# Shift and scale of a conditioned encoder layer in two parts of 512 features, the first six W_in blocks in two halves of K

## What is computed

```
mod = (silu(c) @ w_mod + b_mod).reshape(B, 6, 1, D)
shift1, scale1, gate1 = mod[:, 0], mod[:, 1], mod[:, 2]
h  = layer_norm(x) * (1 + scale1) + shift1
z  = h @ w_in + b_in            # [u | v | pool | gates], 5 * 1024 columns
v  = gelu(z_v) ...
```

## Time and profile before

| | us |
|---|---|
| median of 3 runs | 949.63 |
| lowest, highest | 948.38, 950.42 |
| the profiled execution | 948.7 |
| its span, first to last instruction | 947.0 |
| PE busy | 897.3 (95%) |
| DVE, ACT, POOL busy | 379.0, 241.4, 114.2 |
| mean granted clock of TensorE | 0.990 |

### The profile page before, as it was taken

The page is one execution under the profiler, slowest core; times in us unless marked ns, Lnnn a source line. Parts: engine busy times, 40 slices in busy tenths (PEclk is TensorE's granted clock), DMA queues, the critical chain, the costliest instruction groups (busy, mean ns, idle before and its releaser), DMA issues. The chain is left out here.

```text
span 947.0 us, 11855 instructions
## 1 busy us (share of the span) xinstructions
PE 897.3 (95%) x4416; PEld 543.0 (57%) x4416; DVE 379.0 (40%) x647; ACT 241.4 (25%) x351; POOL 114.2 (12%) x143
## 2 busy tenths in 40 slices
PE   3999999999999999999999999999888999999994
PEld 2577766888888888787544444344344344444431
DVE  4533443466344236788622323132121232222346
ACT  2422243441234235345511111011010011101113
POOL 2120366000001000000000000000000010000041
PEclk9999999999999999999999999999998999999998
DMA  9985755356464722807999999999999999999994
GB/s 369 357 269 183 265 190 183 118 190 253 178 225 157 219 89 89 300 11 310 401 385 415 425 420 428 421 428 424 427 424 420 414 405 425 423 427 423 424 415 144
DMA packets 53126, 295.27 MB, mean 312 GB/s; under 512 B 5606, under 2 KB 7750, under 8 KB 33602
## 3 DMA queue, kind: packets, MB, share of 16 engines
q1 hardware_dynamic: 42752, 263.47, 69.3%
q0 software_dynamic: 9824, 29.80, 9.3%
q10 hardware_dynamic: 482, 1.13, 0.3%
HBM read 275.81 MB, written 22.83 MB: 315 GB/s over the span
## 5 line engine op out<-in xcount | busy, mean ns | idle before, releaser
L674 PE MATMUL banks<-down_w,hid_t 128*64 128x512 f32 x512 | 118.5, 599 | 10.7 <-issue 5.9
L674 PE MATMUL banks<-h_hi,w_hi 128*128 128x512 f32 x320 | 124.8, 390 | 0.3 <-ACT h_hi L1287 0.3
L674 PE MATMUL banks<-h_hi,w_lo 128*128 128x512 f32 x320 | 124.7, 390 | 0.0
L674 PE MATMUL banks<-h_lo,w_hi 128*128 128x512 f32 x320 | 124.6, 397 | 0.0
L674 PE MATMUL banks<-up_w,x_by_expert 128*64 128x512 f32 x256 | 112.5, 592 | 0.0
L674 PE MATMUL banks<-gate_w,x_by_expert 128*64 128x512 f32 x256 | 112.5, 592 | 0.0
L674 PE MATMUL banks<-gate_w,x_by_pair 128*64 128x512 f32 x240 | 105.5, 592 | 0.1
L674 PE MATMUL banks<-up_w,x_by_pair 128*64 128x512 f32 x240 | 105.5, 592 | 0.0
L1673 DVE TENSOR_TENSOR w_lo<-raw,w_hi 128x1024 fp32r<-128x1024 f32 x56 | 68.5, 1225 | 77.2 <-ACT w_hi L1253 77.1
L1493 ACT ACTIVATE sg_hid<-banks 64x512 f32<-64x512 f32 x33 | 19.5, 591 | 311.6 <-PE banks L674 311.6
L2019 DVE TENSOR_TENSOR sg_hid<-banks,sg_hid 64x512 f32<-64x512 f32 x32 | 22.2, 694 | 183.8 <-ACT sg_hid L1493 183.7
(11 more groups left out here) (325 smaller groups left out, 1304.6 us busy)
## 6 DMA issues: line engine op xcount, KB each, us to landing
down_w<-in_w_exp_down SPq DMA_DIRECT2D x64, 1024.0 KB, 18.2
gate_w<-in_w_exp_gate SPq DMA_DIRECT2D x28, 2048.0 KB, 21.1
up_w<-in_w_exp_up SPq DMA_DIRECT2D x28, 2048.0 KB, 25.6
modraw<-in_w_mod SPq DMA_DIRECT2D x24, 1024.0 KB, 7.7
raw<-in_w_in SPq DMA_DIRECT2D x9, 2048.0 KB, 9.8
round_y<-zrow POOLq DMA_DIRECT2D x6, 2048.0 KB, 7.7
gate_w<-in_w_exp_gate SPq DMA_DIRECT2D x6, 1024.0 KB, 9.5
up_w<-in_w_exp_up SPq DMA_DIRECT2D x6, 1024.0 KB, 12.0
```

Of the source, the lines that this page charges most:

```text
L674: return pe.matmul(out, lhsT, rhs, start=start, stop=stop, skip_group_check=True)
```

## The change

The 1024 features of shift1 and scale1 are computed in two parts of 512.

- W_mod's first 2048 columns are loaded in two rounds of eight loads (first_mod_source): part 0 takes columns 0 to 511 of shift and of scale for all 1024 rows, part 1 columns 512 to 1023. A load is 512 KB in runs of 2 KB. Behind part 0 come the chunks 0 to 3 of W_in unit 0 (in two pieces of 256 columns) and of unit 1; behind part 1 the chunks 4 to 7 of both.
- A modulation unit (first_mod_unit) handles two chunks of rows; a part has four units of four products each. Even and odd chunks are summed in different rows of MOD, and VectorE adds the two when it takes the columns (first_scales). So 16 + 16 products stand where 32 stood, and two sets of column transposes where one stood. They go to bank 7.
- h is formed for chunks 0 to 3 behind part 0, and for 4 to 7 behind part 1 (H_VECTOR = 2, 0, 6, 4; H_POOL = 1, 3, 5, 7; H_ORDER is gone).
- Blocks 0 to 5 are summed in six banks, first over chunks 0 to 3, then over 4 to 7. Their splits use four half buffers. TensorE's order: pair of blocks 0 and 1 over part 0; unit (1,0); block 2; unit (1,1); block 3; units (1,2) and (1,3); block 4; columns of part 1; block 5; the pair over part 1; then the loop n = 0 to 7, in which blocks 2 to 5 have only their second half.
- On VectorE the copy of the parameters' columns (pcol) moves behind the scaling of x; the silu waits for TensorE directly. b_mod comes by 12 DMAs instead of 8. One keep_clock(512) stands between units (0,2) and (0,3), where three stood around units 6 and 7.

```diff
-            for m in range(KC):
-                if m == 6:
-                    sp.dma_start(raw[:, 0, :, 0:256], unit_source(0)[:, :, 0:256]).then_inc(s_wfirst, 16)
-                sp.dma_start(modraw0[m][:, :, :], mod_source(m)).then_inc(s_m0[m], 16)
-            sp.dma_start(raw[:, 0, :, 256:512], unit_source(0)[:, :, 256:512]).then_inc(s_w[0], 16)
-            load_unit(1)
+            for part in range(2):
+                for kc in range(KC):
+                    m = 4 * part + kc // 2
+                    landed = s_m0[4 + kc // 4 if part else kc // 2]
+                    sp.dma_start(modraw0[m][:, kc % 2, :, :], first_mod_source(part, kc)).then_inc(landed, 16)
+                chunks = slice(PART * part, PART * part + PART)
+                if part == 0:
+                    for c in range(2):
+                        cols = slice(256 * c, 256 * c + 256)
+                        sp.dma_start(raw[:, 0, chunks, cols], unit_source(0)[:, chunks, cols]).then_inc(s_wpre[c], 16)
+                    sp.dma_start(raw[:, 1, chunks, :], unit_source(1)[:, chunks, :]).then_inc(s_wpre[2], 16)
+                else:
+                    for u in range(2):
+                        sp.dma_start(raw[:, u, chunks, :], unit_source(u)[:, chunks, :]).then_inc(s_w[u], 16)
...
+            def first_mod_unit(part, q):
+                if part == 0:
+                    pe.wait_ge(s_m0[q], 32)
+                else:
+                    pe.wait_ge(s_m0[4 + q // 2], 64)
+                for k in range(2):
+                    for v in range(2):
+                        j = 2 * v + k
+                        x = mm(MOD[32 * j:32 * j + 32, :], silu_c[:, 2 * q + k, :], modraw0[4 * part + q][:, k, v, :], start=(q == 0), stop=(q == 3))
+                x.then_inc(pe_mod, 1)
...
-            mod_units0(0, 2)
+            first_mod_unit(0, 0)
+            first_mod_unit(0, 1)
...
-            mod_units0(2, KC)
+            first_mod_unit(0, 2)
+            keep_clock(512)
+            first_mod_unit(0, 3)
             keep_clock(256)
             pe.wait_ge(act_nt, 2 * TILES)
...
+            part_pair(0)
+            first_mod_unit(1, 0)
+            part_block(0, 2)
+            first_mod_unit(1, 1)
+            part_block(0, 3)
+            first_mod_unit(1, 2)
+            first_mod_unit(1, 3)
+            part_block(0, 4)
+            pe.wait_ge(dve_col, 1)
+            first_mod_columns(1)
+            part_block(0, 5)
+            part_pair(1)
             for n in range(8):
-                if n >= 2:
+                if 2 <= n < FIRST:
+                    part_block(1, n)
+                elif n >= FIRST:
                     block_at(n, n % 2, h_hi, h_lo, act_z, n - 1)
...
-            dve.wait_ge(pe_pro, 1)
-            dve.tensor_copy(pcol[:, :], COL[:, 0:64]).then_inc(dve_pro, 1)
...
+            first_mod_rows(0)
+            first_scales(0)
+            dve.wait_ge(dve_col, 2)
+            first_split_lo(0)
+            first_split_lo(1)
+            for kc in H_VECTOR[0:2]:
+                modulated(kc)
+            for kc in range(PART):
+                h_low(kc)
+            for b in range(2, FIRST):
+                first_split_lo(b)
+            first_mod_rows(1)
+            split_lo(0)
+            split_lo(1)
+            first_scales(1)
+            dve.wait_ge(dve_col, 4)
+            for kc in H_VECTOR[2:4]:
+                modulated(kc)
+            for kc in range(PART, KC):
+                h_low(kc)
```

More of the change, by code:

```diff
@@ L211, in hybrid_encoder @@
         s_sgu_w = sem("s_sgu_w")
-        s_wfirst = sem("s_wfirst")
+        s_wpre = [sem(f"s_wpre{i}") for i in range(3)]
         s_bmod = sem("s_bmod")
-        s_m0 = [sem(f"s_m0_{i}") for i in range(KC)]
+        s_m0 = [sem(f"s_m0_{i}") for i in range(6)]
         s_m = [sem(f"s_m{i}") for i in range(2)]
@@ L371, in mod_source, with first_mod_source, halves_of_chunks, bank_of @@
             return w_mod[0, kc * 128:kc * 128 + 128, r * 2048:r * 2048 + 2048].rearrange("p (j n) -> p j n", j=4)
+        def first_mod_source(part, kc):
+            return w_mod[0, 128 * kc:128 * kc + 128, 0:2048].rearrange("p (v f n) -> p v f n", v=2, f=2)[:, :, part, :]
+        def halves_of_chunks(tiles, turn):
+            first = PART * (turn // 2 % 2)
+            return tiles[turn % 2][:, first:first + PART, :]
+        def bank_of(b):
+            return B[(2, 3, 4, 5, 0, 1)[b]] if b < FIRST else Z[b % 2]
         def gate_src(w, e):
@@ L686, in keep_clock, with first_mod_columns @@
                 mm(B[4][:, 0:w], ident, cst[:, 0:w])
[L688 to L693, removed]
+            def first_mod_unit(part, q):
[4 more added lines that the diff above has]
+                for k in range(2):
+                    for v in range(2):
+                        j = 2 * v + k
+                        x = mm(MOD[32 * j:32 * j + 32, :], silu_c[:, 2 * q + k, :], modraw0[4 * part + q][:, k, v, :], start=(q == 0), stop=(q == 3))
+                x.then_inc(pe_mod, 1)
+            def first_mod_columns(part):
+                pe.wait_ge(dve_row0, part + 1)
+                for k in range(4):
+                    x = pe.transpose(COL[:, 128 * k:128 * k + 128], modrow_first[:, part, 128 * k:128 * k + 128], ident)
+                x.then_inc(pe_modcol, 1)
             pe.wait_ge(act_pro, 1)
-            mod_units0(0, 2)
+            first_mod_unit(0, 0)
+            first_mod_unit(0, 1)
             for i in range(TILES):
@@ L1280, in _, with h_high @@
                          B[2 * (i % 2) + hb][:, :].rearrange("p (k n) -> p k n", k=4)).then_inc(act_nt, 1)
[L1281 to L1295, removed]
+            def h_high(part):
+                for kc in range(PART * part, PART * part + PART):
+                    if kc % PART == 0:
+                        act.wait_ge(dve_col, 2 * part + 2)
+                        for r in range(REQ):
+                            x = act.activation(h_hi[:, kc, SEQ * r:SEQ * r + SEQ], n_t[:, kc, SEQ * r:SEQ * r + SEQ], ACT.Identity,
+                                               scale=scale1p[:, kc, r:r + 1], bias=mod_t[:, 0, kc, r:r + 1])
+                    elif kc in H_POOL:
+                        act.wait_ge(pool_aff, H_POOL.index(kc) + 1)
+                        x = copy(h_hi[:, kc, :], h32[:, kc, :])
+                    else:
+                        act.wait_ge(dve_aff, H_VECTOR.index(kc) + 1)
+                        x = copy(h_hi[:, kc, :], h32[:, kc, :])
+                    x.then_inc(act_hhi, 1)
+            part_split_hi(0, 0)
+            part_split_hi(0, 1)
+            h_high(0)
+            for b in range(2, FIRST):
+                part_split_hi(0, b)
+            part_split_hi(1, 0)
+            part_split_hi(1, 1)
+            h_high(1)
             def run(seg, n, evac=None):
@@ L1690, in modulated, with h_low @@
                 x.then_inc(dve_aff, 1)
-            def h_low(done, kc):
+            def h_low(kc):
                 if kc in H_POOL:
```

157 lines of the change are left out of this document (99 added, 58 removed).

## The result

| | before | changed |
|---|---|---|
| median of 13 runs each, us | 948.29 | 953.31 |
| lowest, highest | 946.79, 950.58 | 950.12, 957.48 |
| ratio to before (95% interval) | | 1.0051 (1.0037 to 1.0065) |
| the profiled execution, its span | 948.7, 947.0 | 957.48, 955.8 |

The changed kernel is 5.0 us slower. I had forecast 0.6 us slower, and a range that ended at 953.0.

What follows compares the result with a forecast made beforehand. TensorE, busy 95% of the span, was taken as the bound. 8.7 us gained minus 5.1 moved work, 3.1 stall and 1.1 clock gave 0.6 us slower, 950.2 us, with a range of 945.5 to 953.0.

Steps and rivals of the forecast that it cites:

- First W_in matmul at 28.9: In the front, TensorE's first W_in matmul was to start at 28.9 us instead of 37.63.
- 28.1 to 29.7: Sign to look for in the front: the first W_in matmul starting within these times, in us.
- Gain: In the front, W_in's earlier start was to bring 8.7 us, between 8.0 and 9.5.
- with all transposes at half clock: Low case for the front: the transposes of x run at half clock with late data, gaining 8.0 us.
- 5.1 us moved into the dense stretch: Part 1's modulation units 4.0, column transposes 0.5, changes of matmul kind 0.4 and late h_lo 0.2, moved among W_in matmuls.
- before they are wanted: In the front, GpSimd's chunks 1 and 3, at 1.17 us each, were to be ready before TensorE needs them.
- h_lo would be late by 0.2: At the end of the first pair of blocks, TensorE was to wait 0.2 us for the fourth h_lo.
- The stall: TensorE waits 3.1 us (0 to 3.8) at modulation unit 2 for load 10, which shares DMA engines with GpSimd's loads.
- The rival of no stall: Modulation load 10 lands within 7.8 us, so TensorE never waits; 3.6 us faster, 946.0; chance 0.23.
- The clock, 1.1: After TensorE's wait for modulation load 10, its granted clock falls briefly, costing 1.1 us, between 0 and 2.5.
- The front's sum, -0.6: 8.7 gained, less 5.1 moved work, 3.1 waiting and 1.1 lower clock: 0.6 us slower.
- I carry a shift of the front to the end one to one.: Everything after the front is chained to TensorE by semaphores, so any front shift reaches the kernel's end at full size.

Runs made afterwards that it cites:

- e4_loads_behind: The changed kernel with GpSimd holding back the b_spatial and router loads until modulation load 10 has landed; 954.21 us, ratio 1.0067.
- e9_spatial_early: The changed kernel with w_spatial's load sent earlier, ahead of a nearly idle DMA stretch, and the router's loads behind the pooling branch; 948.14 us, ratio 1.0009.
- e10_spatial_early_padded: The changed kernel with w_spatial's load earlier, router's loads later, and idle waits up to 128 instructions per engine (not TensorE) over the kernel before; 945.64 us, ratio 0.9977.
- e2_delay2: The kernel before with 5 more clock-keeping products on TensorE ahead of the first W_in matmul; 949.75 us, ratio 1.0021.
- e3_delay4: The kernel before with ten more products of 512 columns on TensorE ahead of the first W_in matmul; 951.86 us, ratio 1.0044.
- e5_before_padded: The kernel before with only already-met waits added: 11, 11, 6 and 10 instructions on ScalarE, VectorE, GpSimd and SyncE; 951.53 us, ratio 1.0037.
- e8: The changed kernel with GpSimd's loads later, modulation loads ahead of W_in units, and idle waits to 128 instructions per engine (not TensorE) over before; 949.2 us, ratio 1.0007.
- e7: The changed kernel with GpSimd's loads waiting for modulation load 12, router's loads later, and modulation loads ahead of W_in units; 950.21 us, ratio 1.0031.
- the padded changed kernel: The changed kernel with idle waits up to 128 instructions over the kernel before on each engine but TensorE, measured twice; 953.33 and 951.39 us, ratios 1.0047 and 1.004.
- e11_before_padded128: The kernel before with 128 more instructions of already-met waits on each of ScalarE, VectorE, GpSimd and SyncE; 947.7 us, ratio 0.9999.

## Why the prediction was wrong

Its steps, in order.

- **First W_in matmul at 28.9.** It came at 29.32, inside the 28.1 to 29.7 named. The transposes began at 17.71 (17.8 forecast), unit (0,3) at 24.84 (24.5), and from there to W_in it took 4.48 us (4.4). The 0.4 us lie mostly under the transposes, 17.71 to 22.79, 5.1 us instead of 4.8: they follow one another 0.21 us apart until 19.3 and 0.11 apart from there, and ScalarE's evacuation holds them once (0.39 at 20.81). The windows show a clock of 1.00 throughout; that the slow pace is the lower clock I take from rows 6, where the granted clock is 0.50 and the pace the same (the 7 matmuls counted there overlap; they are 4.7 a us, not the 7 of my text). Gain 8.3 instead of 8.7. This gain is that of the changed kernel's first profile. In the nine traces with this front the pace rises between 19.3 and 22.2 and the first W_in matmul comes at 29.32 to 30.45, in six of them behind the 29.7 that I had named as the latest, with a gain down to 7.2. Where the clock rises, which I had said that no row shows, varies by execution, and my 8.0 "with all transposes at half clock" was not the worst case: 32 of them 0.21 apart would take 6.8 us, 2.0 more than my 4.8. (A small slip beside it: of the 8 MB between the first and the last unit, one is W_in's, so that 2.53 us per MB is not a rate of 8 KB runs alone.)
- **5.1 us moved into the dense stretch.** This term was too small; it is 6.0: from the first W_in matmul to block 6 it was 41.86 us and is 52.15; less 2.65 and 1.6 for wait and clock, 47.9. The four units take 3.84 (4.0 forecast) and the columns 0.35 (0.5). Too little was allowed for two things: the wait at 31.09 for chunk 1 (0.56, with 0.17 more around it), for which I had written that GpSimd's chunks come "before they are wanted", and the changes between kinds of matmul, which come at both ends of each unit and each half block and not four times; about 1.1 us are left for them. That h_lo would be late by 0.2 did not happen: 33.94 has no wait.
- **The stall.** GpSimd's w_spatial load went out 3.2 us into the second pair (3.0 forecast), load 10 at 58.9, 7.2 us into it (7.0 to 7.1), and landed at 69.2, 17.5 us into it (18.0). The wait was 2.65 instead of 3.1. This step held in each of its parts. e4_loads_behind, e9_spatial_early and e10_spatial_early_padded bear out its cause: with part of GpSimd's loads out of the way the wait was 1.14, 0.31 and 0.88. Whether the amount of data or its short runs count was not tried.
- **The rival of no stall.** Its rule of the Trainium skill ("DMA: Bandwidth & Descriptors", Queues, rings and completion order), by which the queues take turns, made it likelier to me than it was. The load took 10.3 us beside GpSimd's loads, 8.0 and 8.6 with fewer of them: whatever the turns, what the other queue still holds lengthens it.
- **The clock, 1.1.** It cost 1.6. The granted clock was at 0.50 from about 70.5 to 73.9, half as long as in my row of comparison at 723, which had lost 2.5.
- **The front's sum, -0.6.** 8.3 - 6.0 - 2.65 - 1.6 = -1.95, and block 6 is 1.98 us late (the 6.0 is what the other terms leave). The moved work (0.9), the clock (0.5) and the gain (0.4) were each estimated too favourably, the stall (0.45) too unfavourably: 1.4 us in all.
- **"I carry a shift of the front to the end one to one."** This is the step that failed. For the shift itself it is true (e2_delay2 and e3_delay4). But it took for granted that unchanged code far behind the change costs the same. It does not: the change also moved that code by 11, 11, 6 and 10 instructions, and this alone costs 3.5 us in the kernel before (e5_before_padded), 3.0 (e10 against e9) or 2.3 (e8 against e7, 1.0 by the medians) in edited forms of the changed one. 2.0 from the front and about 3 from the place of the code make the 5.0 measured; my sum and its bound of 953.0 had no term for the second.

What is open. That the place costs time is shown by the times; the traces show one site (behind expert 18's further round: VectorE late by "issue", hid_t late, and the instruction packets, in all six traces of kernels with the small shift, in none of the eight others). But the stretch there is only 0.2 to 3.1 us longer than the 24.18, 1.0 in the trace of e5_before_padded, so that most of its 3.5 us have no row. That instructions are fetched there is argued from the packets and the idle time; no run changes the fetch itself. Which of the four engines has to be at its place was not tried. The front of the changed kernel may also lose more than 2.0 us in executions in which the clock rises later, so that the split into 2.0 and 3 is not exact. Nor is it explained why the padded changed kernel gained only 0.4 to 1.0 us.

## What to carry to other kernels

Before a loss or a gain of a few tenths of a per cent is put down to an edit, make the kernel before with the same number of idle instructions added on each engine; if it moves too, it is the place of the code. Then look at where the shift between two traces grows, not only at the edited stretch. And when a load is late because of another queue's loads, look for an idle stretch ahead: bytes held back return later, as e4_loads_behind and e7_loads_late showed, while in e9_spatial_early 0.5 MB sent ahead, with the router's small loads far behind, made no later unit wait. A front in one trace is one sample as well: look in several for a start that varies.

## What the runs showed of the hardware

38 instructions without any work made the kernel 0.37% slower, and 512 made no difference. The part of the delay that has rows stands behind the one further round of an expert, where VectorE sits idle 5.9 to 7.0 us by "issue" and six packets of the instruction queue pass between the data transfers.

The Trainium skill ("Runtime: NRT & Kernel Launch", Instruction fetch mechanics) says that an engine streams its instructions in blocks of 256 ahead of use, at a cost that is mostly hidden, but that a taken branch to code outside the blocks it holds must fetch first. The further round stands in a branch on a count, and VectorE's idle time behind it (6.40 us in the changed kernel, none in the kernel before) agrees with the second half of that; no run here shows the size of a block, only that lists longer by 128 behave as the old ones.

A wait does not tell by its length alone whether the clock falls: it fell behind the 2.65 us of unit 2 here and held behind the 1.14 us in e4_loads_behind and the 1.94 us in e7_loads_late, but at expert 17 it fell behind 1.22 us in e7_loads_late, held behind 1.21 us in e10_spatial_early_padded, and held behind 2.73 us in e11_before_padded128.
